# A two-block transformer kernel on one core: first unit by its weights' highs, last norms' scales by logarithm and exponential, output in four parts, reordered FFN ends, direct column sums at the joins

## The reference

```python
def first_block(x, ...):                      # DEPTH = 4
    for i in range(4):
        xn = rmsnorm(x, norm_g[i, 0])
        m = (attention, gating, s5_layer, attention)[i](xn, ...)
        x = x + m
        x = x + conv_gated_ffn(rmsnorm(x, norm_g[i, 1]), ffn_w_up[i], conv_w[i], conv_b[i], w_down[i])
    return rmsnorm(x, final_norm_g)

def conv_gated_ffn(xn, w_up, conv_w, conv_b, w_down):   # D_FF = 2816
    h = causal_depthwise_conv(xn @ w_up, conv_w, conv_b)  # three taps along the tokens
    a, g = jnp.split(h, 2, axis=-1)
    return (jax.nn.silu(g) * a) @ w_down

def second_block(x, c, ctx, ...):             # DEPTH_2 = 1
    h = modulate(rmsnorm_2(x, g_norm_mix), sh1, sc1)
    x = x + gt1 * token_mixer(h, hc, ...)
    h2 = modulate(rmsnorm_2(x, g_norm_ffn), sh2, sc2)
    x = x + gt2 * ((silu(h2 @ w_gate) * (h2 @ w_up)) @ w_down)   # same width, no convolution
    return rmsnorm_2(x, g_final)
```

## Time and profile before

| what | value |
|---|---|
| time, median of 3 runs | 1774.53 us (1773.03 to 1775.22) |
| the profiled execution's own time | 1772.18 us |
| its span in the profile | 1770.4 us |
| TensorE busy | 1687.0 us, 95% |
| DVE, ACT, GpSimd busy | 1234.8, 847.8, 128.9 us |
| mean granted TensorE clock | 0.983 |
| loaded from HBM | 284 MB |

### The profile page before, as it was taken

One profiled execution on the slowest core, in us unless ns is written; L12 is line 12 of the kernel. 1 busy time (PEld: TensorE's weight loads), 2 busy tenths in 40 slices (PEclk: granted clock), 3 DMA queues, 4 the chain that ended last, 5 costly groups with the idle time before them and its releaser, 6 DMA issues.

```text
span 1770.4 us, 34592 instructions
## 1 busy us (share of the span) xinstructions
PE 1687.0 (95%) x14451; PEld 1596.4 (90%) x14451; DVE 1234.8 (70%) x1573; ACT 847.8 (48%) x972; POOL 128.9 (7%) x112
## 2 busy tenths in 40 slices
PE   6999999999999999899999999999989999989997
PEld 6989999898999996699999998999988568889997
DVE  5857777786887758857777785787775576654444
ACT  5455555636445541355454545555554534344333
POOL 1002000103500052100000100100000000000000
PEclk9999999999999999999999999999989999999999
DMA  7804555535445523444545680554542032145451
GB/s 297 334 34 158 190 186 187 185 127 190 164 168 182 191 103 121 153 173 152 190 172 185 251 330 28 184 184 177 190 143 96 24 119 96 49 143 190 175 181 71
DMA packets 40051, 286.51 MB, mean 162 GB/s; under 512 B 4576, under 2 KB 4576, under 8 KB 5664
## 3 DMA queue, kind: packets, MB, share of 16 engines
q1 hardware_dynamic: 39024, 280.99, 44.0%
q10 hardware_dynamic: 944, 4.33, 0.7%
HBM read 284.25 MB, written 1.05 MB: 161 GB/s over the span
## 4 chain that ended last, share of the span: by engine, by line
PE 66%; DVE 15%; ACT 9%; issue 6%; POOL 1%; DMA 1%; DVEq 0%; ACTq 0%; POOLq 0%; SPq 0%
PE PS L1810 19%; PE PS L1811 18%; PE PS L1812 18%; ACT whi L387 5%; DVE wlo L943 4%; DVE AR L1168 4%; ACT AR L499 2%; PE PS L2081 1%; POOL AR L2602 1%; PE PS L2059 1%; PE PS L2095 1%; PE PS L2457 1%; DVE XL L987 1%; PE PS L2219 1%; PE PS L2379 1%
## 5 line engine op out<-in xcount | busy, mean ns | idle before, releaser
L1810 PE MATMUL PS<-XH,whi 128*128 128x256 f32 (+1 forms) x2696 | 785.4, 291 | 17.0 <-DVE wlo L943 8.3
L1811 PE MATMUL PS<-XL,whi 128*128 128x256 f32 (+1 forms) x2696 | 775.6, 288 | 0.0
L1812 PE MATMUL PS<-XH,wlo 128*128 128x256 f32 (+1 forms) x2696 | 775.1, 288 | 0.0
L943 DVE TENSOR_TENSOR wlo<-raw,whi 128x2048 fp32r<-128x2048 f32 x240 | 555.7, 2318 | 178.4 <-ACT whi L387 178.3
L1810 PEld LDWEIGHTS PS<-XH,whi 128*128 128x128 f32 x2696 | 519.1, 193 | 29.5 <-issue 14.2
L1811 PEld LDWEIGHTS PS<-XL,whi 128*128 128x128 f32 x2696 | 519.8, 193 | 4.6 <-issue 0.2
L1812 PEld LDWEIGHTS PS<-XH,wlo 128*128 128x128 f32 x2696 | 519.5, 193 | 4.1
L387 ACT ACTIVATE whi<-raw 128x2048 fp32r<-128x2048 f32 x240 | 455.9, 1902 | 59.8 <-PE PS L1812 42.2
L1810 PE MATMUL PS<-HH,whi 128*128 128x256 f32 x880 | 251.5, 286 | 12.8 <-DVE HL L1188 8.6
L1811 PE MATMUL PS<-HL,whi 128*128 128x256 f32 x880 | 250.4, 285 | 0.0
L1812 PE MATMUL PS<-HH,wlo 128*128 128x256 f32 x880 | 250.3, 284 | 0.0
(11 more groups left out here) (375 smaller groups left out, 1510.9 us busy)
## 6 DMA issues: line engine op xcount, KB each, us to landing
raw<-wst SPq DMA_DIRECT2D x248, 1024.0 KB, 4.8
AR<-mst SPq DMA_DIRECT2D x17, 1024.0 KB, 6.5
XT<-x_in SPq DMA_DIRECT2D x2, 512.0 KB, 5.9
AR<-crow ACTq DMA_DIRECT2D x2, 512.0 KB, 5.9
AR<-sbc ACTq DMA_DIRECT2D x1, 1024.0 KB, 6.8
AR<-ctxin ACTq DMA_DIRECT2D x1, 1024.0 KB, 6.0
y_out<-XT SPq DMA_DIRECT2D x1, 1024.0 KB, 3.9
AR<-sgw ACTq DMA_DIRECT2D x1, 512.0 KB, 3.6
```

Of the source, the lines that this page charges most:

```text
L943: dve.tensor_tensor(wlo[:, r, :], raw[:, u % RING, :], whi[:, r, :].bitcast(F32), ALU.subtract)\
L1810: pe.matmul(dst, sh, mh, start=first, stop=False, **kw)
L1811: pe.matmul(dst, sh, ml, start=False, stop=False, **kw)
L1812: return pe.matmul(dst, sl, mh, start=False, stop=last, **kw)
```

## The change

What it does:

- **Start.** Unit 1's load is issued ahead of the constants. ACT makes XH 0 to 3, the highs of unit 0, XH 4 to 7, then the four squares. DVE makes XL and the lows of unit 0 before it waits for the constants. A new `first_unit` does the first unit's products with the highs of the weights first and the 16 with its lows last.
- **Scales.** `rms` takes the logarithm, then exp(−0.5·) on ACT; DVE's reciprocal goes. The table for both is loaded ahead of the last mixer's residual and at the end of the last FFN. This concerns the norms ahead of the last FFN and at the end.
- **Output.** DVE multiplies XT by the gains once its squares are made, then four products of 512 columns by the scale; SP writes four quarters, each when it is ready.
- **FFN's end** (`turned`: all but the fourth). The last ups and downs come as up 18, 19, 20, 21, down 8, 9, 10; the last two pairs of hidden tiles lie in the upper halves of XH and XL (`halves`) and wait for no down unit. The host orders the stream so, and ACT and DVE split it in that order.
- **Direct sums.** At the scales 2, 4 and 6 GpSimd adds only the first three pairs; TensorE takes the fourth pair's two tiles directly. The row sums there come at (m = 1, k = 3) of the next unit; at scale 0 they come at (m = 0, k = 3).
- **Last FFN's up 0** does k outside, m inside.

The diff, cut. The three pieces that begin with `if turned:` stand behind the loops of ACT, DVE and TensorE, in this order; the piece with `not free` is TensorE's `up`.

```diff
+BEHIND_FFN = 2, 4, 6
+        def halves(h, turned):
+            k = 2 * (h - FT // 2 + 2)
+            return (XH[:, k:k + 2, T:2 * T], XL[:, k:k + 2, T:2 * T]) if turned and k >= 0 else (HH[:, :, :], HL[:, :, :])
+        def up_unit(u0, j, turned):
+            return u0 + j if j < 2 else u0 + 2 + 3 * (j // 2 - 1) + j % 2 - (turned and j >= FT - 2)
+        def down_unit(u0, h, turned):
+            return u0 + 4 + 3 * h + (2 if turned and h == FT // 2 - 3 else -2 if h == FT // 2 - 1 else 0)
...
             sp.dma_start(XT[:, 4:8, :], xin[:, 4:8, :]).then_inc(S["x_in2"], 16)
+            sp.dma_start(raw[:, 1, :], wst[1]).then_inc(w_loaded[1], 16)
             sp.dma_start(CST[:, :], cst).then_inc(S["const_in"], 16)
             sp.dma_start(VEC[:, GAINS:], vec[:, GAINS:]).then_inc(S["vec_in"], 16)
-            for u in range(1, RING):
+            for u in range(2, RING):
...
-            sp.wait_ge(S["normed"], 2 * KT)
-            sp.dma_start(out, XT[:, :, :]).then_inc(S["y_out"], 16)
-            sp.wait_ge(S["y_out"], 16)
+            for mp in range(4):
+                sp.wait_ge(S["normed"], KT + mp + 1)
+                sp.dma_start(out[:, 2 * mp:2 * mp + 2, :], XT[:, 2 * mp:2 * mp + 2, :]).then_inc(S["y_out"], 16)
+            sp.wait_ge(S["y_out"], 64)
...
             def rms():
                 act.wait_ge(S["norm_sum"], t.norm + 1)
-                act.activation(RMS, PS[:, 6, 0:T], ACT.Sqrt, bias=vcol("eps", 0), scale=1.0 / D)\
+                act.activation(RMS, PS[:, 6, 0:T], ACT.Ln, bias=vcol("eps", 0), scale=1.0 / D)\
                     .then_inc(S["rms_ready"], 1)
+                act.wait_ge(S["rms_ready"], 2 * t.norm)
+                act.activation(RSTX, RMS, ACT.Exp, scale=-0.5).then_inc(S["rms_ready"], 1)
...
+                if turned:
+                    s1 += 3 * (n - 2)
+                    for h in (n - 1, n):
+                        for j in range(2):
+                            split_hi(s1 + 2 * (h - n + 1) + j)
+                            up(2 * h + j)
+                        hidden(h)
+                    split_hi(s1 + 4)
+                    split_hi(s1 + 5)
...
+                if turned:
+                    s1 += 3 * (n - 2)
+                    for h in (n - 1, n):
+                        for j in range(2):
+                            if conv:
+                                take(2 * h + j)
+                            split_lo(s1 + 2 * (h - n + 1) + j)
+                            up(2 * h + j)
+                        hidden(h)
+                    split_lo(s1 + 4)
+                    split_lo(s1 + 5)
...
+                if turned:
+                    for j in range(2 * n - 2, 2 * n + 2):
+                        up(j)
+                    down(n - 2)
+                    down(n - 1)
                 down(n, last=True)
...
             def norm_stream(name):
+                for mp in range(4):
+                    dve.wait_ge(S["sq_ready"], 4 * t.norm + mp + 1)
+                    for k in (2 * mp, 2 * mp + 1):
+                        ins = dve.tensor_scalar(XT[:, k, :], XT[:, k, :], vcol(name, k), None, ALU.mult)
+                link(ins)
                 rstd()
-                for k in range(KT):
-                    dve.scalar_tensor_tensor(XT[:, k, :], XT[:, k, :], vcol(name, k), RSTX, ALU.mult, ALU.mult)\
-                        .then_inc(S["normed"], 1)
+                for mp in range(4):
+                    x = XT[:, 2 * mp:2 * mp + 2, :]
+                    dve.tensor_tensor(x, x, RSTX.unsqueeze(1).broadcast_to([P, 2, T]), ALU.mult).then_inc(S["normed"], 1)
...
+            def first_unit(b):
+                kw = dict(skip_group_check=True)
+                pe.wait_ge(S["setup"], 1)
+                pe.matmul(PS[:, b, :], ZB[:, 0:P], ZB[:, :], start=True, stop=False, **kw)
+                pe.wait_ge(S["w_hi"], 1)
+                for ks in (range(4), range(4, KT)):
+                    for part, ready in ((XH, "op_hi"), (XL, "op_lo")):
+                        for k in ks:
+                            pe.wait_ge(S[ready], k + 1)
+                            for m in range(2):
+                                pe.matmul(PS[:, b, m * T:(m + 1) * T], whi[:, 0, k * 256 + m * P:k * 256 + m * P + P],
+                                          part[:, k, 0:T], start=False, stop=False, **kw)
+                pe.wait_ge(S["w_lo"], 1)
+                for k in range(KT):
+                    for m in range(2):
+                        mm = pe.matmul(PS[:, b, m * T:(m + 1) * T], wlo[:, 0, k * 256 + m * P:k * 256 + m * P + P],
+                                       XH[:, k, 0:T], start=False, stop=k == KT - 1, **kw)
+                mm.then_inc(S["w_used"], 1)
+                pe.wait_ge(S["setup"], 3)
+                scale_sums(0, 1, 3)
...
-            def scale_sums(unit, m, k, rows=(0, 3)):
+            def scale_sums(unit, m, k):
                 if (unit, m, k) == (0, 1, 3):
-                    t.rows = rows
+                    tiles, t.rows = ((0, 1, 6, 7), (1, 3)) if t.free in BEHIND_FFN else ((0, 1), (0, 3))
                     pe.wait_ge(S["square_sum"], t.free + 1)
+                    if t.free in BEHIND_FFN:
+                        pe.wait_ge(S["square"], 4 * t.free + 4)
...
+                    if j == 0 and not free:
+                        bank = PS[:, 4 + q0 % 2, :]
+                        pe.matmul(bank, ZB[:, 0:P], ZB[:, :], start=True, stop=False, skip_group_check=True)
+                        for kt in range(KT):
+                            operand(True, kt)
+                            for m in range(2):
+                                mm = product(bank[:, m * T:(m + 1) * T], w(slot, kt * 256 + m * P, kt * 256 + m * P + P),
+                                             x(kt), False, kt == KT - 1, skip_group_check=True)
```

More of the change, by code:

```diff
@@ L487, in ffn @@
                 u0, q0, up0, hid0 = t.u, t.pp, t.up, t.hid
+                turned = not (conv and layer == 3)
                 def up(j, it=None):
                     k = 0 if it is None else it
-                    u = u0 + 2 + 3 * (j // 2 - 1) + j % 2 if j >= 2 else u0 + j
+                    u = up_unit(u0, j, turned)
                     if conv:
@@ L511, in hidden @@
                     act.wait_ge(S["hid_ready"] if conv else S["pp_taken"], (up0 if conv else q0) + 2 * h + 2 + 2 * k)
-                    if h > 0:
+                    hh, _ = halves(h, turned)
+                    if h > 0 and not (turned and h >= n - 1):
                         act.wait_ge(S["w_used"], u0 + 2 + 3 * h + 3 * k)
-                    act.activation(HH[:, :, :], HID, ACT.Copy).then_inc(S["hh_ready"], 1)
+                    act.activation(hh, HID, ACT.Copy).then_inc(S["hh_ready"], 1)
                 if conv:
@@ L959, in rstd @@
             def rstd():
-                dve.wait_ge(S["rms_ready"], t.norm + 1)
-                dve.reciprocal(RSTX, RMS).then_inc(S["rstd_ready"], 1)
-                dve.wait_ge(S["rstd_ready"], t.norm + 1)
+                dve.wait_ge(S["rms_ready"], 2 * t.norm + 1)
                 t.norm += 1
@@ L1900, in tokens @@
                 t.u += 1
[L1902 removed]
+            def scale_sums(unit, m, k):
                 if (unit, m, k) == (0, 1, 3):
[L1905 removed]
+                    tiles, t.rows = ((0, 1, 6, 7), (1, 3)) if t.free in BEHIND_FFN else ((0, 1), (0, 3))
                     pe.wait_ge(S["square_sum"], t.free + 1)
+                    if t.free in BEHIND_FFN:
+                        pe.wait_ge(S["square"], 4 * t.free + 4)
                     for c in range(2):
[L1908 removed]
+                        for i in tiles:
                             mm = pe.matmul(PS[:, 6, c:c + 1], SQ[:, i, c * P:(c + 1) * P], ones[:, 0:1],
[L1910 removed]
+                                           start=(i == 0), stop=(i == tiles[-1]))
                     mm.then_inc(S["col_sum"], 1)
@@ L1975, in residual, with ffn @@
                 t.op += KT // per
-            def ffn(aside=None, free=True, then=True):
+            def ffn(aside=None, free=True, then=True, turned=True):
                 u0, q0, hid0 = t.u, t.pp, t.hid
@@ L2598, in square_sums @@
             def square_sums(n):
-                for mp in range(1, 4):
+                last = 2 if n in BEHIND_FFN else 3
+                for mp in range(1, last + 1):
                     pool.wait_ge(S["square"], 4 * n + mp + 1)
                     ins = pool.tensor_tensor(SQ[:, 0:2, :], SQ[:, 0:2, :], SQ[:, 2 * mp:2 * mp + 2, :], ALU.add)
-                    if mp < 3:
+                    if mp < last:
                         link(ins)
@@ L2637, in unit_ffn @@
         order += [up[2 * h:2 * h + 2], down[h - 1:h]]
+    if turned:
+        order[-3:] = order[-2], order[-3], order[-1]
     return np.concatenate(order + [down[-1:]])
```

123 lines of the change are left out of this document (70 added, 53 removed).

## The result

The changed kernel takes **1762.24 us** in the median of 4 runs (1759.41 to 1763.71), the kernel before, run beside it, 1773.9 us: ratio **0.9936**, 95% interval 0.9922 to 0.9949. So 11.7 us were gained, where 17.2 were forecast. The profiled execution took 1759.41 us (span 1757.6), 12.8 us less than the one shown of before. The changed kernel's other three runs were longer by 1.7 to 4.3 us, at a lower mean granted clock (0.982 to 0.986 against 0.988).

The account below looks back on a forecast made before the run. TensorE, busy 95% of the span, was taken as the bound, with gains from shorter pauses. Terms 2.7 + 2.3 + 1.7 + 1.7 + 3.5 + 1.7 + 3.6 = 17.2 us, off the median 1774.53, gave 1757 us; range 1753 to 1761.

Parts of the forecast that it names:

- gain 2.7 us; bounds 1.0 and 3.9: Kernel start: first product near 10.5 us and an earlier unit 1, less a new 1.2 us stop.
- I put its start at 19.6: Start: unit 1 begins at 19.6 us instead of 23.46, after its lows, GpSimd's adds and 0.8 us of sums.
- The second, forecast stop on the diagonal: Within unit 1: TensorE waits 1.2 us because the row sums now stand after 12 products instead of 27.
- Second FFN to state space: Join: 2.0 plus a half-clock stretch's 1.5, minus 0.8 for later row sums and 1.0 for matrices: 1.7 us gained.
- moves the pause, it does not remove it: Three convolution FFNs' ends: the HL wait becomes stops of 0.4 and 1.7 us on lows; 0.3 us lost.
- Joins, 2.3 and 1.7: Joins of first FFN to gating, gain 2.3 us, and third FFN to attention, gain 1.7 us.
- Last norm and up 0, 3.5: Last norm and last FFN's up 0: exponential replaces reciprocal, k outermost; 3.5 us gained, the norm's 1.3 included.
- the case for which the prediction had 4.4: Last FFN's up 0 at full clock ends 4.4 us earlier; 3.4 with 3.41 us at half clock.
- Last FFN 1.7: Last FFN's end: no convolution, so DVE has slack and the HL wait goes wholly, 1.7 us gained.
- Output 3.6: Output: products 0.75, norm 1.3 and last quarter's write 1.5 us less; 3.6 us, bounds 2.0 and 4.1.
- start and last norm give little: Rival: row sums held by DVE's splits at unit 1, clock low 6.8 us again; 1762 us, chance 0.17.
- The clock as a rival for a loss: Rival: moved pauses hold TensorE at 1.2 GHz some 14 us at four FFN ends; 1781 us, chance 0.02.

Follow-up runs that it names:

- the start put back: Changed kernel with its old start: three products per tile, casts ahead of the operand's lows, second unit loaded after the constants; 1762.87 us, ratio 0.9938.
- The kernel with the scales unblocked: Changed kernel with unit 1's lows before the casts, root's table loaded before unit 2's highs, unit 2's lows behind the diagonal; 1757.46 us, ratio 0.9902.
- the kernel with the old sums: Changed kernel with sums of squares behind the FFNs as before: GpSimd makes all three additions, row sums with the next unit; 1763.25 us, ratio 0.9948.
- GpSimd's products later: Changed kernel, but GpSimd's first state-space products wait until VectorE has written the diagonal of that stage's scales; 1757.25 us, ratio 0.9911.
- the kernel with the old order: Changed kernel with the old order of the last units in the first three FFNs; 1761.71 us, ratio 0.9937.

## Why the prediction fell short

Bound and direction were right. Of 17.2 us the medians lack 5.5: 4.4 of them in the profiled executions (12.8 measured), the rest in the runs around them. Two of its seven terms failed; they lack 6.3 us, and the others, 1.9 us better than forecast, did not make up for them.

- **Start, "gain 2.7 us; bounds 1.0 and 3.9": measured 0.3 in the profiled execution, 0.3 to 1.2 against the start put back.** The failed step is "I put its start at 19.6": it took for granted that VectorE is free for unit 1's lows at their highs' end, 16.9 us; unit 1 started at 21.18. The change had moved the casts behind the operand's lows, and with the five small operations they were not in the walk: 2.0 us more, 16.9 to 18.9. The first cast alone took 1.31 us there, 0.46 before. With them out of the way unit 1 started at 19.80. The adds, put at 18 to 19.5, were done at 17.60 and did not matter; the slowing that I gave to them showed on VectorE's lows beside them (1.5 instead of 0.48 us, twice, as it had in before), which still ended at 16.45, ahead of the highs. The Trainium skill (GPSIMD Engine Reference, Specifications), which I had cited for the adds, says that the two engines share their SBUF interfaces and contend; these rows agree. The second, forecast stop on the diagonal was 0.48 us, and 1.1 where the clock did not fall; 1.2 was forecast. Not priced was the fall of the clock behind the first stop, from 22.0 on; against the kernel whose same start had none it cost 0.6 us. The kernel with the scales unblocked had neither stop nor fall: 3.6 us against before, near the upper bound of the forecast.
- **Second FFN to state space, "1.7": measured −2.2 up to the state space's end.** The join's part was 2.0 by the rows of the *first* join, where GpSimd has nothing else to do. Here the add that was taken away let GpSimd's next work start 7.7 us earlier (4.0 of it against the join itself, which had moved by 3.7), beside VectorE's critical chain. The prediction followed TensorE's order at this place and never asked what stands next on GpSimd. Price: 2.7 us, by the kernel with the old sums and by the one with GpSimd's products later alike. The other 1.6 us, within the state space, were a term put at nothing, and their cause is shown in part only. The stops at "issue" move with the length of TensorE's program, which has 72 pieces against 63; seven of the nine come from the FFNs' ends, as the kernel with the old order has 65. That kernel had one stop there and gained 0.4 us. But before had two such stops of its own, at 714.6 and 730.3, with 5.2 us in all against 4.7 after, and other kernels with 72 pieces and two stops each gave −2.6 to +0.5 us in this stage. No row of before was read for these stops.
- **FFN's end, "moves the pause, it does not remove it".** Held in the main: the wait on HL went, and before down 10 TensorE stopped 1.4 us for lows, where 1.7 was walked; the 0.4 before down 9 did not come. Apart from what the start gave, the last down of the first FFN began 0.1 us earlier, where 0.3 later was forecast, and in the second FFN 0.9 us later, for 1.3.
- **Joins, 2.3 and 1.7: 3.0 and 2.3.** The wait of 2.02 us for GpSimd is gone; so are the half-clock stretches behind both. The kernels with the old order and the old sums split the first: 1.4 us by the order, 1.6 by the sums.
- **Last norm and up 0, 3.5: 4.3.** The exponential takes 0.42 us (0.45 forecast). With both edits the clock does not fall there, the case for which the prediction had 4.4; it took the one with a fall.

```profile
1554.16 0.47 ACT L423 ACTIVATE SM<-PS,VEC 128x256 f32<-128x256 f32 x1 [1.22 <-PE PS L2016]
...
1554.66 0.42 ACT L426 ACTIVATE AR<-SM 128x256 f32<-128x256 f32 x1
```

- **Last FFN 1.7: 1.8. Output 3.6: 3.2.** The last write landed in 2.7 us, not 2.4, and the four are not written in turn: they are issued 0.6 us apart and take 2.3 to 2.7 each, and three are under way while VectorE still makes the last quarter. The Trainium skill's advice to coalesce (DMA: Bandwidth & Descriptors, Rules for kernel authors) is for many small transfers and names 64 KB as the size below which overhead prevails; the quarters have 256 KB, so these runs do not speak against it.
- **Of the rivals**, "start and last norm give little" gave the right time, 1762, by luck: the start did give little, but by casts and not by the row sums, the last norm gave more than forecast, and what was lost at the state space is not in it. The clock as a rival for a loss did not come: the falls stayed 3.4 to 10.2 us long.

What stays open: the median of after is 2.8 us above its profiled execution at a lower mean clock, which fits more or longer falls of the clock, but only one execution has its rows. Why the clock fell behind a stop of 1.8 us in two kernels, and not behind one of 1.5 in another, is open: one profiled execution each. That TensorE's program could be laid out so that no stop falls into the state space was not tried.

## What to carry to other kernels

When work is taken from an engine's queue, look at what follows it there: it starts earlier, and where it slows the engine on the critical path it can cost more than was saved; one wait put that right, for 2.7 us at the join. Price a moved start through to the end of the first steady unit, since 4.7 us at the first product were 0.3 us a hundred microseconds later, until the two stops behind it were gone (3.6 us then). Unrolling a loop makes a program longer and moves the stops for its pieces in a later stage of short products; what that costs in all, these runs do not settle. A single profiled execution per variant, read event by event, separates parts that the medians (the runs of one kernel lie 1.5 to 7.7 us apart) cannot; but a part of the time that moves with the clock needs more than one.

## What the runs showed that I had not expected

- VectorE's split of 2048 columns takes 2.29 us alone and 4.0 to 4.5 beside GpSimd's products of 1024 columns; a diagonal of 128 columns takes 0.28 alone and 1.8 to 2.0 beside them; a low of 256 columns takes 0.48 alone, 1.5 beside GpSimd's adds and 2.1 beside its products.
- TensorE's program is loaded in pieces of 16 KB. In the stage of short products TensorE stopped at "issue" for 0.9 to 4.0 us, each time until 2.2 to 2.6 us after the start of a piece's transfer, so it was the piece that it waited for; the stops move with the program's length. The kernel before had them too.
- The clock's fall is a matter of the single execution: the same start with a wait of 1.5 us had none, with one of 1.8 us, in two other kernels, a fall of 3.4 us, and the code of the old start had its products move from 0.21 to 0.12 us apart at 18.5 us in one execution and at 20.4 in another, for 0.9 us. Of nine executions with the changed start's wait of 1.5 us for unit 1's lows, eight had a fall at 21.3 to 22.5 us and one had none.
